# Odd layer of a hybrid trunk: eight attention steps placed behind the last projection tiles

## The reference

```python
qw, kw, vw, qn, kn, vn = jnp.split(p, splits, axis=-1)      # p = u @ w_in
qw = rms_norm(qw, q_norm_win); kw = rms_norm(kw, k_norm_win)
qn = rms_norm(qn, q_norm_na);  kn = rms_norm(kn, k_norm_na)
qwl = apply_axial_rope(qwl, cos, sin); kwl = apply_axial_rope(kwl, cos, sin)
ol = concatenate([window_attention(qwl, kwl, vwl, kwc, vwc, sink_win),
                  neighbourhood_attention(qnl, knl, vnl, knc, vnc, rpb_na)]) @ w_out
```

## Time and profile before

| | us |
|---|---|
| median of 3 runs | 1215.54 |
| lowest, highest | 1215.38, 1216.03 |
| the profiled execution, its own time | 1215.36 |
| its span in the trace | 1213.6 |
| TensorE busy | 1163.3 (96%) |
| VectorE busy | 836.8 (69%) |
| ScalarE busy | 620.7 (51%) |

### The profile page before, as it was taken

How to read it: one execution, slowest core, us unless ns; L and a number is a source line. 1 busy time by engine, 2 the same in 40 slices (tenths; PEclk the granted TensorE clock), 3 DMA queues, 4 the chain that set the end, 5 groups by cost and what they waited for, 6 DMA issues and landing times.

```text
span 1213.6 us, 17212 instructions
## 1 busy us (share of the span) xinstructions
PE 1163.3 (96%) x6430; PEld 933.9 (77%) x6430; DVE 836.8 (69%) x1202; ACT 620.7 (51%) x1080; POOL 86.7 (7%) x73
## 2 busy tenths in 40 slices
PE   5999899999998999999999999999899899999998
PEld 3567677786766787887887887887688569998997
DVE  4563678887976556893882882897758886755555
ACT  5540384848576436621421422446745776754543
POOL 0000101010010033000000000043000004000000
PEclk9999999999999999999999999999999999999999
DMA  9856343332322233643643634641334004556554
GB/s 361 342 217 261 89 127 116 105 122 79 122 79 79 70 120 102 234 156 122 214 150 124 230 132 141 228 130 56 120 105 138 19 1 141 173 191 191 178 187 156
DMA packets 49893, 179.13 MB, mean 148 GB/s; under 512 B 5216, under 2 KB 7584, under 8 KB 47776
## 3 DMA queue, kind: packets, MB, share of 16 engines
q1 hardware_dynamic: 49536, 177.66, 43.1%
q10 hardware_dynamic: 288, 0.56, 0.2%
HBM read 177.05 MB, written 1.15 MB: 147 GB/s over the span
## 4 chain that ended last, share of the span: by engine, by line
PE 78%; DVE 8%; ACT 8%; DMA 3%; issue 3%; SPq 0%; DVEq 0%; ACTq 0%
PE ps L1897 50%; PE ps L1904 9%; PE ps L2191 7%; ACT ey L1246 3%; PE ps L1989 2%; DVE sm L1845 1%; DMA mhalf<-in_w_mod 1%; ACT ey L1249 1%; PE ps L1920 1%; PE ps L2165 1%; DVE prob L1870 1%; ACT cacc L1194 1%; PE ps L2102 1%; PE ps L2148 1%; DMA xload<-in_ctx 1%
## 5 line engine op out<-in xcount | busy, mean ns | idle before, releaser
L1392 DVE TENSOR_TENSOR w_lo<-raw,w_hi 128x1024 fp32r<-128x1024 f32 x206 | 261.3, 1268 | 98.8 <-ACT w_hi L1020 98.6
L1020 ACT ACTIVATE w_hi<-raw 128x1024 fp32r<-128x1024 f32 x206 | 216.9, 1053 | 192.9 <-DMA raw<-in_w_ff 156.4
L1897 PE MATMUL ps<-a_hi,w_hi 128*128 128x512 f32 (+1 forms) x820 | 300.2, 366 | 0.0
L1897 PE MATMUL ps<-a_hi,w_lo 128*128 128x512 f32 (+1 forms) x820 | 289.8, 353 | 0.0
L1897 PE MATMUL ps<-a_lo,w_hi 128*128 128x512 f32 (+1 forms) x820 | 289.4, 353 | 0.0
L1897 PEld LDWEIGHTS ps<-a_hi,w_hi 128*128 128x128 f32 x820 | 156.1, 190 | 25.2 <-issue 2.7
L1897 PEld LDWEIGHTS ps<-a_lo,w_hi 128*128 128x128 f32 x820 | 156.1, 190 | 23.3 <-issue 1.0
L1897 PEld LDWEIGHTS ps<-a_hi,w_lo 128*128 128x128 f32 x820 | 155.8, 190 | 21.4
L1897 PE MATMUL ps<-b_hi,w_hi 128*128 128x512 f32 x304 | 119.2, 392 | 0.0
L1897 PE MATMUL ps<-b_lo,w_hi 128*128 128x512 f32 x304 | 118.5, 390 | 0.0
L1897 PE MATMUL ps<-b_hi,w_lo 128*128 128x512 f32 x304 | 118.3, 389 | 0.0
(11 more groups left out here) (289 smaller groups left out, 1768.4 us busy)
## 6 DMA issues: line engine op xcount, KB each, us to landing
raw<-in_w_ff SPq DMA_DIRECT2D x128, 512.0 KB, 3.5
mring<-in_w_mod SPq DMA_DIRECT2D x32, 768.0 KB, 5.1
raw<-in_w_in_even SPq DMA_DIRECT2D x36, 512.0 KB, 5.8
mring<-in_w_mod SPq DMA_DIRECT2D x16, 1024.0 KB, 6.7
ey<-acum_rows SPq DMA_DIRECT2D x32, 384.0 KB, 5.0
raw<-in_w_in_odd SPq DMA_DIRECT2D x18, 512.0 KB, 3.4
mhalf<-in_w_mod SPq DMA_DIRECT2D x16, 512.0 KB, 9.6
raw<-in_w_out_even SPq DMA_DIRECT2D x16, 512.0 KB, 3.5
```

What stands on the lines that cost most here:

```text
L1020: nc.scalar.activation(w_hi[:, u % RING, :, :], raw[:, u % RING, :, :], ACT.Copy).then_inc(hi_done, 1)
L1392: v.tensor_tensor(w_lo[:, u % RING, :, :], raw[:, u % RING, :, :], w_hi[:, u % RING, :, :].bitcast(F32), ALU.subtract).then_inc(lo_done, 1)
L1897: ins = mm(out_ap, w_[:, n % RING, k, :], (x_[k][:, 0:ntok] if type(x_) is list else x_[:, k, 0:ntok]), start=(k == 0 and j == 0), stop=(k ...
```

## The change

`ODD` gets another order, with query tiles and value tiles in turn at its end. From the tenth tile on, one attention step is placed behind each tile: `attend(j)` puts S, max and exp of step j + 1, PT of step j and O of step j - 1 behind the tile, and scale of step j + 1 directly behind them, ahead of the next tile's weight split on VectorE. From step 8 on the order is the old one. `dup` moves two tiles further back. Since tiles hold banks 0 and 1 meanwhile, S of steps 0 to 8 uses banks 4 and 5 alone; the `hstat` steps of kn.3 and all qn use bank 7, and the outputs of all head pairs but 4 and 6 use bank 6. Waits on all rotations, norms and value tiles at once become waits on the one that a step reads. prob and pT move to other addresses, and the first four output pairs are split into arrays of their own, since tiles still read a_hi and a_lo.

The diff, without the hunks that only place arrays and name them:

```diff
@@ -88,11 +88,12 @@
 
 ODD_AT = {"qn": (768, SEQ), "kn": (1280, T), "qw": (0, SEQ), "kw": (512, T)}
 ODD = [(kind, int(i), ODD_AT[kind][0] + P * int(i), ODD_AT[kind][1]) if kind != "v" else ("v", int(i), 640 if i == "0" else 1664 + P * int(i), T)
-       for kind, i in (q.split(".") for q in ("v.0 kw.0 kn.0 kn.1 v.1 qw.0 qw.1 v.2 qw.2 qw.3 kn.2 qn.0 qn.1 kn.3 qn.2 qn.3 v.3 v.4").split())]
+       for kind, i in (q.split(".") for q in ("v.0 kw.0 kn.0 kn.1 qw.0 qw.1 kn.2 qw.2 qw.3 kn.3 v.1 qn.0 v.2 qn.1 v.3 qn.2 v.4 qn.3").split())]
 
 NORM_FF0, NORM_MIX1, NORM_FF1 = ("norm", 0, "ff"), ("norm", 1, "mix"), ("norm", 1, "ff")
 LEADS = [NORM_FF0, NORM_MIX1, NORM_FF1]
 LEAD_BANKS = (4, 5)
+FIRST_STEP, BESIDE = 10, 8
 HOISTED = 3
 HI_ON_ACT = (0, 1, 2, 4, 6)
 MOD_AFTER_LEAD = (3, 4, 6, 7, 8, 9, 10, 11)
@@ -286,28 +287,36 @@
         if m:
             s.append(("vrow", NORM_FF0, m - 1))
     s += [NORM_FF0, ("lead", NORM_FF0), ("mlp", 0), NORM_MIX1, ("lead", NORM_MIX1)]
-    for n in range(len(ODD) + 3):
-        if n == len(ODD) - 1:
-            s.append(("S", 0))
+
+    def attend(j):
+
+        if j == BESIDE:
+            s.append(("S", j + 1))
+        if j < BESIDE:
+            order = [("S", j + 1), ("PT", j), ("max", j + 1), ("O", j - 1), ("exp", j + 1)]
+            if j >= 2 and j % 2 == 0:
+                order += [("ohi", j // 2 - 1), ("olo", j // 2 - 1)]
+        else:
+            order = [("S", j + 2), ("ohi", (j - 2) // 2), ("max", j + 1), ("scale", j), ("olo", (j - 2) // 2), ("exp", j + 1), ("PT", j), ("O", j - 1)]
+        for kind, i in order:
+            if kind in ("ohi", "olo"):
+                if j < BESIDE or j % 2 == 1:
+                    s.append((kind, i))
+            elif 0 <= i < len(ATTN):
+                s.append((kind, i))
+    for n in range(FIRST_STEP + len(ATTN) + 1):
+        if 0 <= n - FIRST_STEP < BESIDE:
+            s.append(("scale", n - FIRST_STEP))
         if n < len(ODD):
             gemm(*ODD[n][:2])
-        if n == len(ODD) - 1:
-            s.append(("max", 0))
-
         behind = lambda back: [o[:2] for i, o in enumerate(ODD) if max(i, 1) == n - back]
         for back, stage in ((1, "hstat"), (2, "hnorm"), (3, "rot")):
             s.extend((stage,) + o for o in behind(back) if o[0] != "v" and (stage != "rot" or o[0][1] == "w"))
         s.extend(("vtok", o[1]) for o in behind(1) if o[0] == "v")
-        s.extend(("dup",) for o in behind(4) if o[0] == "kw")
-    n = len(ATTN)
-    for j in range(-1, n + 1):
-        for kind, i in (("S", j + 2), ("ohi", j - 2), ("max", j + 1), ("scale", j), ("olo", j - 2), ("exp", j + 1), ("PT", j), ("O", j - 1)):
-            if kind in ("ohi", "olo"):
-                if i >= 0 and i % 2 == 1:
-                    s.append((kind, i // 2))
-            elif 0 <= i < n and (kind, i) != ("max", 0):
-                s.append((kind, i))
-    s += [("ohi", n // 2 - 1), ("olo", n // 2 - 1)]
+        s.extend(("dup",) for o in behind(6) if o[0] == "kw")
+        if n >= FIRST_STEP - 1:
+            attend(n - FIRST_STEP)
+    s += [("ohi", len(ATTN) // 2 - 1), ("olo", len(ATTN) // 2 - 1)]
     s += [("grow",), ("vprep", NORM_FF1)]
     for m in range(KT):
         gemm("outO", m)
@@ -476,7 +485,7 @@
         elif k == "cb":
             job(st, B_AUX[0])
         elif k == "hstat":
-            job(st, B_AUX[n_aux % 2], freed=("hv_done", nk))
+            job(st, B_AUX[n_aux % 2 if st[1:] != ("kn", 3) and st[1] != "qn" else 1], freed=("hv_done", nk))
             n_aux += 1
         elif k == "yoff":
             for i, (q, none) in enumerate((("f", SCAN_F[0]), ("b", SCAN_B[0]))):
@@ -491,13 +500,13 @@
             job(st + (1,), B_TR, freed=("kd_done", 2))
         elif k == "S":
             for par in range(2):
-                job(st + (par,), (B_SEG, B_GEMM[0])[st[1] % 2] + par)
+                job(st + (par,), (B_SEG, B_GEMM[0])[st[1] % 2 if st[1] > BESIDE else 0] + par)
         elif k == "PT":
             for par in range(2):
                 job(st + (par,), (B_TR, B_AUX[0])[par], freed=("pT_done", 2 * st[1] + par + 1))
         elif k == "O" and st[1] % 2 == 0:
             t = st[1] // 2
-            job(("Opair", t), (B_Y, B_AUX[1])[t % 2], freed=("split_done", 5 * KT + t + 1), filled=("pv_done", 4 * t + 4))
+            job(("Opair", t), B_AUX[1] if t >= 4 and t % 2 == 0 else B_Y, freed=("split_done", 5 * KT + t + 1), filled=("pv_done", 4 * t + 4))
     steps_of = lambda kind: [q for q in steps if q[0] == kind]
     gemms = steps_of("gemm")
     n_even = sum(g[1] in ("conv", "fn", "z", "outA", "outB") for g in gemms)
...
@@ -2333,9 +2350,10 @@
                     t, qt = ATTN[i]
                     if i == 0:
                         pe.wait_ge(kd_done, 2)
-                        pe.wait_ge(rope_done, len(rot_n))
-                    if t == 4:
-                        pe.wait_ge(qn_done, len(hn_n))
+                    if qt == 0 and t < 4:
+                        pe.wait_ge(rope_done, rot_n[("rot", "qw", t)] + 1)
+                    if qt == 0 and t >= 4:
+                        pe.wait_ge(qn_done, hn_n[("hnorm", "qn", t - 4)] + 1)
                     for par in range(2):
                         if free_before[st + (par,)]:
                             pe.wait_ge(*emptied(st + (par,)))
@@ -2357,8 +2375,8 @@
                     i = st[1]
                     t, qt = ATTN[i]
                     pe.wait_ge(pT_done, 2 * i + 2)
-                    if i == 0:
-                        pe.wait_ge(vtok_done, 5)
+                    if qt == 0:
+                        pe.wait_ge(vtok_done, 1 if t < 4 else t - 2)
                     if i % 2 == 0:
                         if free_before[("Opair", t)]:
                             pe.wait_ge(*emptied(("Opair", t)))
```

More of the change, by code:

```diff
@@ L615, in trunk @@
         vtok = place("vtok", [P, NCH, 5 * P])
+        vtok_end = at[0]
         at[0] = max(at[0], region + 2 * 16384)
@@ L623, in trunk @@
         bias = place("bias", [P, 2, 8, SEQ], offset=region + 16384)
-        prob = place("prob", [P, 3, 2, T], offset=region + 32768)
-        pT = place("pT", [P, 2, 2, T], offset=region + 32768 + 12288)
+        prob = place("prob", [P, 3, 2, T], offset=macc_at + 7680)
+        pT = place("pT", [P, 2, 2, T], offset=vtok_end)
+        assert vtok_end + 8 * 2 * T <= region + 16384
+        o_hi = place("o_hi", [P, 4, SEQ], F32R, offset=hr_at)
+        o_lo = place("o_lo", [P, 4, SEQ], F32R, offset=hr_at + 4 * 4 * SEQ)
         fin = place("fin", [P, 2, D], offset=out_at)
@@ L652, in trunk @@
         mix_hi = [mixE[:, 0, k, :] if k < 2 else a_hi[:, k, :] for k in range(KT)], [b_hi[:, k, :] for k in range(KT)]
+        attn_hi = [o_hi[:, k, :] if k < 4 else a_hi[:, k, 0:SEQ] for k in range(KT)]
+        attn_lo = [o_lo[:, k, :] if k < 4 else a_lo[:, k, 0:SEQ] for k in range(KT)]
         mix_lo = [mixE[:, 1, k, :] if k < 2 else a_lo[:, k, :] for k in range(KT)], [b_lo[:, k, :] for k in range(KT)]
@@ L727, in operands @@
                 return mix_hi[half], mix_lo[half]
+            if st[1] == "outO":
+                return attn_hi, attn_lo
             return a_hi, a_lo
@@ L1380, in _ @@
                     act.wait_ge(*filled(("Opair", st[1])))
-                    nc.scalar.activation(a_hi[:, st[1], 0:SEQ], ps[:, b, 0:SEQ], ACT.Copy).then_inc(signal(ohi_done), 1)
+                    nc.scalar.activation(attn_hi[st[1]], ps[:, b, 0:SEQ], ACT.Copy).then_inc(signal(ohi_done), 1)
         @block.vector
@@ L1874, in _ @@
                     b, _ = jobs[("Opair", t)]
-                    v.tensor_tensor(a_lo[:, t, 0:SEQ], ps[:, b, 0:SEQ], a_hi[:, t, 0:SEQ].bitcast(F32), ALU.subtract).then_inc(signal(split_done), 1)
+                    v.tensor_tensor(attn_lo[t], ps[:, b, 0:SEQ], attn_hi[t].bitcast(F32), ALU.subtract).then_inc(signal(split_done), 1)
                 elif k == "out":
```

## The result

The change makes the kernel slower: 1221.88 us (median of six runs, 1219.23 to 1224.21) against 1215.82 us (1215.38 to 1216.16) before, a ratio of 1.0046 [1.0033, 1.006]. That is outside the predicted range, 3.4 us above its upper end, on the side to which the prediction gave 0.22. The times also scatter by 5 us where the six of before, taken beside them, scatter by 0.8. The longer series of the kernel before that stand beside the experiments (15 to 27 runs) scatter by 3.0 to 3.7, so the contrast is smaller than these first six make it; the scatter is part of the answer all the same.

What follows compares the result with a forecast made beforehand. TensorE's work bounds both halves, so only 17.2 us of idle time could be won. Work of 120.15 plus new and remaining waits made 136.9 us for the part, a change of -0.2: 1215.3 us, range 1211.6 to 1218.5.

Steps and rivals of the forecast that it cites:

- the side to which the prediction gave 0.22: Whole kernel: slower than before by more than 0.2%, 2.4 us; chance 0.22.
- The part's limits: From 861.14 to 998.49 us, 137.35 us: 120.1 of TensorE work, the other 17.2 lost and all there is to win.
- the walk of the three queues: Following the three in-order queues with the profile's durations through the part: 136.9 us, error about 0.5.
- The list of new waits: TensorE waits added: head 2.4, dup.1 2.8, kn.3 statistics 1.7, PT.1 0.4, O.0 3.2, S.10 2.6, PT.9 1.8 us.
- Moving dup: Key copy with two more tiles ahead: removes its 5.6 us wait and 3.0 us of cold clock; dup.1 then waits 2.8.
- The 21.7 us from maximum 11 to the output projection: Tail of the part: the same length, 21.7 us, in old and new order.
- The new gaps: New TensorE waits of 1.7 to 3.2 us, with work around them: clock stays up, no slow clock in the sum.
- The second rival: Clock falls at one new gap (867 to 869.5, 915 to 918 or exit), costing 3.0 us: 1218.3 us; chance 0.12.
- The first: Rival: one bank wait, most likely O.0's 3.2 us near 915 us, does not form: 1212.1 us; chance 0.22.
- The third: Rival: the step chain in short slots overruns its 0.9 us spare, three or four slots losing 0.8 each: 1218.2; chance 0.08.
- The fourth: Rival: tiles would not cover the attention steps; the time of now plus the head's 2.4 us; chance 0.02.
- The rule on transposes: Skill's claim that transposes do not count as clock activity like matmuls; by it the exit slows, 1218.3 us; prediction doubted it.

Runs made afterwards that it cites:

- experiment 4: Kernel before the change, with only dup moved two tiles later: 1209.52 us, ratio 0.9945.
- Experiment 2: Changed kernel with twelve unread products filling the kept wait ahead of O.0: 1219.26 us, ratio 1.0026 against the kernel before.
- experiment 6: Changed kernel with short unread products inside its five large waits (head, dup.1, kn.3 statistics, O.0, S.10): 1218.31 us, ratio 1.0022 against the kernel before.
- experiment 7: Changed kernel with the rotation of qw.3 ahead of the norm of kn.3, and the other four large waits filled: 1215.77 us, ratio 1.0003 against the kernel before.
- experiment 8: Changed kernel with another tile order and two steps beside tiles in place of eight: 1207.86 us, ratio 0.9936 against the kernel before.
- experiment 1: Changed kernel with the rotation of qw.3 ahead of the norm of kn.3 on VectorE, removing O.0's wait: 1216.84 us, ratio 1.0002 against the kernel before.
- experiment 9: Changed kernel with all sixteen steps behind the last tile, its six largest waits filled with unread products: 1215.58 us, ratio 1.0002 against the kernel before.
- Experiment 10: The changed kernel unaltered, run once more (the second sample): 1220.22 us, ratio 1.0037 against the kernel before.

## Why the prediction was wrong

**What held.** The part's limits, the price of each piece, and the walk of the three queues: each wait came at its place and within 0.6 us of its size, and the trace without falls and switches is 137.6 us for 136.9. The list of new waits was complete, and so was the claim that they outweigh those removed. Moving dup was priced at 5.6 + 3.0 less what stays; alone, where 0.8 stay, that is 7.8, and the part of experiment 4 is 7.3 shorter, its time 6.3. The 21.7 us from maximum 11 to the output projection held as well (983.03 to 1004.73).

**The step that failed** is that of the clock: "The new gaps (1.7 to 3.2 us, with work right around them) look like that stretch, not like the two of dup, ... so the sum has no slow clock." I read one row, 940 to 950 us with 5.56 of 10 busy at 1.00, as what a scattered gap does, and carried it to single gaps up to two and a half times as long as the longest in it (1.3 us). The nearest row was dup.1's 3.66 us (the prediction's 3.9 stands in no row), which did bring a fall. Experiment 2 shows that the gap at O.0 alone cost 2.4 us by the clock, and the traces show falls behind gaps of 2.7, 3.1, 3.4 and, in experiments 6 to 8, 1.7 us. The new gaps lay between the two rows, and each of them should have had a chance of its own, priced from both. The same step is in the credit: the prediction took the whole 3.0 us of dup's slow clock as won, while 2.7 us of dup.1's wait stayed and with them a fall that costs 1.5. What the runs show in place of a term of nothing is 4.15 us of slow clock on the path of the first trace, 4.0 by experiment 2.

**The second rival was the mechanism, and it was mis-sized twice.** It had a chance of 0.12 and the price of one fall, 3.0 us; there were three, two of them on the path with 4.15 us. One of these two, behind dup.1, was not in its list of places. And its base was the forecast's. With 4.15 and 0.8 added to the walk the part is 141.9 long, and the trace has 142.6; the last 0.7 is near the walk's own error of 0.5.

**The term that was missing** is the 0.2 us of a tile that directly follows S or O, 0.8 us on the path beside the falls. It could be read before: the one such tile of the old order, behind S.0, took 5.68 where the tile ahead of S.0 took 5.46. The chain of the kernel before:

```profile
927.02 5.46 PE ps L1897 x24
...
933.98 5.68 PE ps L1897 x24
```

**The other rivals.** The first, O.0's wait not forming, did not occur; made to occur (experiment 1) it gave 5.0 us (3.4 against the second sample), more than its 3.2, since the fall went with it. The third, lateness in the short slots, is refuted: there is no wait of O in the middle, and the chain has only TensorE pieces from 921 to 963 us. The fourth is refuted by the waits.

**The rule on transposes.** The prediction set the Trainium skill ("TensorE: Matmul & The Clock Gate", part 4) against the row of 940 to 950. The fills of experiments 2, 6 and 9 are plain products and kept the clock up; no run here filled a gap with transposes, so whether these count is still open. The same page of the Trainium skill says of the start of a kernel that the number of matmuls at the lower clock varies between runs of one kernel (Part 1, "What's actually happening"). Experiment 10 shows the like for falls in mid-kernel: at 870, 892 and 922 us in one execution, at 889, 920 and 978 in the other. I had not used it, and it would have made a range wider than one fall.

**What stays open.** How many falls an execution has on average: a trace shows one execution, and that of experiment 9 lies 1.1 us under its kernel's median. So the split of experiment 9 (6.1 and 2.2) is good to about 1 us. Why gaps of 2.7 and 2.1 us passed without a fall in one execution, and one of 1.7 us did not in three others, no run shows. The 0.2 us per switch is read from the traces and was not undone by a run of its own.

## What to carry to other kernels

When a reordering turns many short waits of TensorE into a few of 2 to 3 us, the sum of the waits is not the cost: price each such gap with a clock fall (here 1.5 to 3 us on the path), and look for the row of the nearest gap, not for one of the same mean activity. Before interleaving two phases, try the cheapest part of the change alone; here one step moved by two tiles brought 6.3 us, and all the rest cost 12.4. Where a gap cannot be removed, unread products in it are a quick test of whether the clock is what it costs, and at O.0 they seem to pay by themselves.

## What the runs showed that I had not expected

- A fall's place is not fixed by the program: two executions of one kernel, with the same gaps, had three falls each, two at the same waits and one at another (889, 920, 978 against 870, 892, 922 us).
- Gaps of 1.7 us, with waits or short products close by, were enough in experiments 6, 7 and 8, while in experiment 2 gaps of 2.7 us at dup.1 and 2.1 us at S.10 passed without a fall in the profiled execution.
- Filling with products nobody reads can gain time: against the first sample of the changed kernel -2.6 us with 12 of them at one wait and -3.6 over five waits, against the second -1.0 and -1.9.
- The kernel with more long gaps has the wider scatter: 6.2 us in eleven runs of the changed kernel, 3.0 to 3.7 in each series of 15 to 27 runs of the kernel before, 1.7 in five runs of experiment 4.
